# Further tiles moved between experts 15 and 16, the last norm done tile by tile, the lower bias ahead of the turned rows

## The chip, the cores and the metric

One core of a Trainium2 chip runs the whole kernel. The metric is the device time of one execution in microseconds, as the median of several runs. Engines: PE (TensorE), DVE (VectorE), ACT (ScalarE), POOL (GpSimd), SP (SyncE, which only issues DMAs here).

## The reference

One transformer layer over 256 prompt tokens and 8 sample tokens: a norm, a projection, a recurrent branch and a sparse attention branch, a merge into x, and a mixture of 32 experts; then a last norm. Only the end matters here (all float32; x is 264 rows of 1,024):

```python
def clamped_swiglu(u):
    glu = jnp.minimum(u[..., :D_FF], SWIGLU_LIMIT)
    lin = jnp.clip(u[..., D_FF:], -SWIGLU_LIMIT, SWIGLU_LIMIT)
    return glu * jax.nn.sigmoid(SWIGLU_ALPHA * glu) * (lin + 1.0)
...
    def expert_chunk(args):                      # one expert, its rows xc
        xc, e = args
        return clamped_swiglu(xc @ w_up[e] + b_up[e]) @ w_down[e] + b_down[e]
...
    return x + moe_ffn(rms_norm(x, norm_ffn), w_router, b_router, w_up, b_up, w_down, b_down)
...
    y_prompt = rms_norm(xp, norm_final)
    y_sample = rms_norm(xs, norm_final)
```

Each token goes to 4 of the 32 experts, weighted. w_up[e] is 1,024 x 2,048 (8 MB), w_down[e] 1,024 x 1,024 (4 MB).

## The kernel before

`build` runs three stages: `rwkv`, `attend`, `experts`. The first two end near 470 us. `experts` calls `expert_tiles` (L2099), in which each engine has its own program, ordered by semaphores.

**One expert.** 64 slots hold the rows of one expert. The 64 rows of 1,024 are halved over the partitions. POOL gathers the rows (`gather`, L2188), PE turns them into bank 6 (`turn_x`, L2417), DVE multiplies them by the norm's gain (`gained_x`, L2287). `up` (L2444) opens banks 0 and 1 with the bias (L2452, chosen by the one-hot tile `pick_up`), then adds eight k-steps of matmuls (L2469). DVE clamps and multiplies with ACT's sigmoid (`tile`, L2312 to L2321), PE turns the result (`turn_h`, L2425), ACT copies it to SBUF as hT (L2224). `down` (L2475) opens bank 4 with its bias (L2483) and adds eight k-steps (L2490). ACT copies bank 4 to y (`rows`, L2230). `comb` (L2431, matmuls at L2440) scatters y back over the 264 tokens into six banks, and DVE adds these to x (`adds`, L2296, at L2303). x has three tiles: 0 and 1 with 128 rows of the prompt, 2 with the 8 samples.

**Weights.** A ring of eight slots of 2,048 KB. Slots 0 to 3 hold w_up of one expert, 4 and 5 w_down of even experts, 6 and 7 of odd ones. SP issues the transfers in the order of use (L2141, L2152), each as soon as PE has used what the slot held: the first upper quarter of expert e+1 when `up(e)` is a quarter done.

**Two orders.** Up to expert 15 (`LATE` = 16) PE does up(e), turn_x(e+1), down(e-1), with comb(e-2) inside up(e). From expert 16 on it does up(e), comb(e-1), turn_x(e+1), turn_h(e), down(e), and up(e) waits for the adds of comb(e-2).

**Further tiles.** An expert with more than 64 rows has further tiles. `each` (L2119) loads their count on every engine (`more_of`, L2116, recorded at L2117), and jumps over a block (branch at L2121) if it is 0. The block holds one tile's code twice (first tile, and the loop over the others). It stands behind expert 31, and PE waits for all adds (`added` >= 192) ahead of it. In the profiled execution no instruction of the block shows up.

**Last norm.** Behind the block: DVE clears the sums; ACT squares each tile with a sum (L2268) and takes the root (L2272); DVE multiplies by the gain (L2391), forms the mean (L2395), the reciprocal (L2399) and the product (L2400); SP writes each tile out (L2177).

Of the kernel before, what the change touches and what calls it, by code (L numbers as in the profile page):

```python
# [25 lines left out]
ALU = mybir.AluOpType  # L26
# [3 lines left out]
P = 128  # L30
D = 1024
# [20 lines left out]
MORE = 16  # L52
# [52 lines left out]
def build(nc, a, o, scratch):  # L105
    ctx = ExitStack()
    with ctx:
# [73 lines left out]
        def slot_of(k):  # L181
            return pairs[k // 2][:, k % 2, :]
# [1916 lines left out]
        def expert_tiles(B, S, st, sp_routes, pool_routes, act_routes, dve_routes, pe_routes, gains, dve_routes_more, pool_routes_more, pe_routes_more):  # L2099
# [11 lines left out]
            sq_out, z = ([slot_of(3 * i + t)[:, 0:D] for t in range(3)] for i in range(2))  # L2111
            ss = sb(st, "final_ss", [P, 3])
            sq, ms, root, y_ok = (sem("fin_" + n) for n in ("squares", "ms", "root", "y_ready"))
            x_ok = Signal("fin_x_ready")
# [4 lines left out]
            def each(eng, tile, count=None, routes_more=None):  # L2119

                with eng.If((more_of(eng) if count is None else count) > 0):  # L2121
                    if routes_more is not None:
                        routes_more(eng)
                    tile(0, eng.value_load(over[0:1, MORE:MORE + 1], min_val=0, max_val=NEXP - 1), True)
                    with eng.Fori(1, MORE) as c:
                        tile(c, eng.value_load(over[0:1, bass.ds(c + MORE, 1)], min_val=0, max_val=NEXP - 1), False)

            with nc.Block() as block:
                @block.sync
                def _(sp):  # L2130
# [30 lines left out]
                    with sp.Fori(2, NEXP // 2) as pair:  # L2161
                        for half in range(2):
                            up(2 * pair + half, True)
                            down(2 * pair + half, half, True)
# [7 lines left out]
                    sp.wait_ge(S["down_done"], NEXP)  # L2172
                    each(sp, further)
                    for t, (t0, n) in enumerate(TILES):
                        sp.wait_ge(y_ok, t + 1)
# [7 lines left out]
                def _(pool):  # L2183
# [19 lines left out]
                    with pool.Fori(1, NEXP - 1) as e:  # L2203
                        gather(e + 1, e + 1, True)
# [10 lines left out]
                    pool.wait_ge(S["x_turned"], NEXP)  # L2215
                    each(pool, further, None, pool_routes_more)

                @block.scalar
                def _(act):
# [26 lines left out]
                    with act.Fori(LATE, NEXP - 1) as e:  # L2246
                        sigmoid(e)
                        turned_h(e)
                        rows(e, True)
                    sigmoid(NEXP - 1)  # L2250
                    turned_h(NEXP - 1)
                    rows(NEXP - 1, True)

# [9 lines left out]
                    each(act, further)  # L2263
                    nc.scalar.activation(root_in[:], ident[:, 0:1], ACT.Sqrt)
                    act.wait_ge(x_ok.sem, 1)

                    def squares(t, n):
                        nc.scalar.activation(sq_out[t][0:n], x[0:n, t, :], ACT.Square, accum_out=ss[0:n, t:t + 1]).then_inc(sq, 1)  # L2268

                    def rooted(t, n):  # L2270
                        act.wait_ge(ms, t + 1)
                        nc.scalar.activation(ss[0:n, t:t + 1], ss[0:n, t:t + 1], ACT.Sqrt).then_inc(root, 1)  # L2272

                    (_, n0), (_, n1), (_, n2) = TILES
                    squares(0, n0)
                    squares(1, n1)
                    rooted(0, n0)
                    squares(2, n2)
                    rooted(1, n1)
                    rooted(2, n2)  # L2280

                @block.vector
                def _(dve):
# [28 lines left out]
                    def tile(e):  # L2312
# [9 lines left out]
                        pick_upper(e + 1)  # L2322
# [21 lines left out]
                    with dve.Fori(LATE, NEXP - 1) as e:  # L2344
                        pick_lower(e)
                        tile(e)
                        gained_x(e + 1)
                        adds(e - 1, True, late_banks)
                        back(e)
                    pick_lower(NEXP - 1)  # L2350
                    tile(NEXP - 1)
                    adds(NEXP - 2, True, late_banks)
                    back(NEXP - 1)
# [32 lines left out]
                    each(dve, further, more_tiles, dve_routes_more)  # L2386
                    step = stepper(dve, dve_chain)
                    step(nc.vector.memset(ss[:], 0.0), x_ok)

                    def gained(t, n):  # L2390
                        step(nc.vector.tensor_tensor(z[t][0:n], x[0:n, t, :], gain[0:n, :], ALU.mult))  # L2391

                    def mean(t, n):
                        dve.wait_ge(sq, t + 1)
                        nc.vector.tensor_scalar(ss[0:n, t:t + 1], ss[0:n, t:t + 1], 1.0 / D, NORM_EPS, ALU.mult, ALU.add).then_inc(ms, 1)  # L2395

                    def scaled(t, n):
                        dve.wait_ge(root, t + 1)
                        step(nc.vector.reciprocal(ss[0:n, t:t + 1], ss[0:n, t:t + 1]))  # L2399
                        nc.vector.tensor_scalar(x[0:n, t, :], z[t][0:n], ss[0:n, t:t + 1], None, ALU.mult).then_inc(y_ok, 1)  # L2400

                    (_, n0), (_, n1), (_, n2) = TILES
                    gained(0, n0)
                    mean(0, n0)
                    gained(1, n1)
                    mean(1, n1)
                    scaled(0, n0)
                    gained(2, n2)
                    mean(2, n2)
                    scaled(1, n1)  # L2410
                    scaled(2, n2)

                @block.tensor
                def _(pe):
# [60 lines left out]
                    def down(e, pair, half, wait, late=False):  # L2475
                        pe.wait_ge(S["hT_ready"], e + 1)
# [31 lines left out]
                    with pe.Fori(2, LATE // 2) as pair:  # L2508
# [10 lines left out]
                    def expert(e, pair, half, more):  # L2519
                        up(e, True, 0, True)  # L2520
                        comb(e - 1, True, late_banks, e + 1)
                        if more:
                            turn_x(e + 1)
                        turn_h(e)
                        down(e, pair, half, True, True)

                    with pe.Fori(LATE // 2, NEXP // 2 - 1) as pair:
                        for half in range(2):
                            expert(2 * pair + half, pair, half, True)
                    expert(NEXP - 2, NEXP // 2 - 1, 0, True)  # L2530
                    expert(NEXP - 1, NEXP // 2 - 1, 1, False)
                    comb(NEXP - 1, True, late_banks, NEXP)
# [36 lines left out]
                    pe.wait_ge(S["added"], 6 * NEXP)  # L2569
                    each(pe, further, None, pe_routes_more)  # L2570
# [44 lines left out]
```

## Time and profile before

| | |
|---|---|
| time, median of 3 runs | 1432.77 us (1429.39 to 1432.85) |
| span of the profiled execution | 1427.3 us |
| PE busy | 1334.0 us (93%) |
| DVE, ACT, POOL busy | 495.5, 189.9, 102.5 us |
| expert matmuls, L2469 and L2490 | 462.0 and 230.2 us |
| HBM read, rate over the span | 478.60 MB, 341 GB/s |
| mean granted clock of PE | 0.981 |

The time of the profiled execution itself isn't known beside its span; the median of the runs is 5.4 us longer than the span. Times in the rows count from the start of the span. Busy shares are averages over three stages with different limits, so the rows are read by stretch. A "q" behind an engine's name is its sequencer, "ld" PE's weight load. L-numbers are lines of the kernel before.

### The profile page before, as it was taken

The numbers are of one execution on the slowest core, as the hardware profiler recorded it, in microseconds if no ns is written. First come the engines' busy times: TensorE is split into PE (matmuls) and PEld (weight loads), VectorE is DVE, ScalarE is ACT, GpSimd is POOL, SyncE is SP. The second block draws the span as 40 slices with busy tenths as digits, with TensorE's granted clock in tenths as the row PEclk, the third lists the DMA queues.
The fourth block names the chain that finished last, engine by engine and source line by source line (L and its number), as shares of the span: only waits on it lengthen the run. The fifth ranks groups of instructions, "written<-read, shape, count | busy, mean of one in ns | idle before, by whom it ended". The sixth has DMA issues, their size and how long they took to land.

```text
span 1427.3 us, 20650 instructions
## 1 busy us (share of the span) xinstructions
PE 1334.0 (93%) x8399; PEld 663.1 (46%) x8400; DVE 495.5 (35%) x1055; ACT 189.9 (13%) x407; POOL 102.5 (7%) x150
## 2 busy tenths in 40 slices
PE   6998889999899999999999999999999999999995
PEld 5887867787688533333333333333333333332331
DVE  3455556434551413223222232224222322233224
ACT  3221112323310300000000000000000000000001
POOL 1002032330000000000000000000000000000000
PEclk9999999999999899999999999999999999999998
DMA  6333248183579799999999999999999999999993
GB/s 212 121 93 92 64 104 270 60 301 111 185 256 369 310 424 430 430 430 430 431 432 430 432 430 431 430 432 427 433 432 431 431 431 432 431 432 430 432 428 141
DMA packets 87027, 479.94 MB, mean 336 GB/s; under 512 B 12740, under 2 KB 52918, under 8 KB 62008
## 3 DMA queue, kind: packets, MB, share of 16 engines
q1 hardware_dynamic: 78664, 452.00, 77.9%
q0 software_dynamic: 7600, 25.45, 5.0%
q10 hardware_dynamic: 704, 1.63, 0.3%
q8 instruction: 46, 0.75, 0.2%
q14 instruction: 13, 0.11, 0.0%
HBM read 478.60 MB, written 8.56 MB: 341 GB/s over the span
## 4 chain that ended last, share of the span: by engine, by line
PE 32%; DMA 32%; DVE 1%; ACT 1%; issue 1%; SPq 0%; DVEq 0%; ACTq 0%
DMA ring<-in_w_up 32%; PE bank L2469 19%; PE bank L2490 7%; PE bank L2440 2%; PE bank L2452 1%; PE bank L2483 1%; PE bank L2422 1%; DVE x L2303 1%; PE bank L2428 0%; PE bank L2072 0%; DVE ring L2391 0%; ACT ex_work L1901 0%; ACT x L1898 0%; DVE x L2400 0%; PE bank L238 0%
## 5 line engine op out<-in xcount | busy, mean ns | idle before, releaser
L2469 PE MATMUL bank<-ring,ex_work 128*64 128x512 f32 x2032 | 462.0, 604 | 23.0 <-DMA ring<-in_w_up 23.0
L2469 PEld LDWEIGHTS bank<-ring,ex_work 128*64 128x64 f32 x2032 | 141.2, 138 | 329.9 <-issue 285.2
L2490 PE MATMUL bank<-ring,ex_work 128*64 128x512 f32 x1024 | 230.2, 603 | 0.0
L2314 DVE TENSOR_SCALAR ex_work<-bank 128x512 f32<-128x512 f32 x32 | 22.1, 692 | 402.0 <-PE bank L2469 402.0
L2303 DVE TENSOR_TENSOR x<-bank,x 128x512 f32<-128x512 f32 (+1 forms) x192 | 117.2, 670 | 101.0 <-PE bank L2440 101.0
L2490 PEld LDWEIGHTS bank<-ring,ex_work 128*64 128x64 f32 x1024 | 71.5, 138 | 156.5 <-issue 156.5
L2440 PE MATMUL bank<-ex_work,ex_back 64*128 64x512 f32 x384 | 91.1, 606 | 1.5 <-ACT ex_work L2234 1.5
L578 PE MATMUL bank<-hT,w_group 128*128 128x264 f32 (+1 forms) x400 | 90.1, 387 | 0.0
L578 PEld LDWEIGHTS bank<-hT,w_group 128*128 128x128 f32 (+1 forms) x400 | 74.3, 186 | 14.7 <-issue 0.7
L2196 POOL DMA_INDIRECT ex_work<-scratch_h,ex_si x31 | 31.8, 1025 | 601.5 <-PE bank L2422 600.6
L2228 ACT ACTIVATE ex_work<-ex_work 128x512 f32<-128x512 f32 x32 | 20.1, 630 | 385.7 <-DVE ex_work L2314 385.7
L1381 PE MATMUL bank<-hT,w_cmp 128*128 128x264 f32 x256 | 65.3, 398 | 0.0
L2440 PEld LDWEIGHTS bank<-ex_work,ex_back 64*128 64x128 f32 x384 | 34.4, 186 | 57.8 <-issue 49.7
L2310 DVE COPY ex_pick_down<-ex_pick 64x64 f32 (+1 forms) x31 | 5.8, 188 | 159.0 <-PE bank L2490 159.0
L2234 ACT ACTIVATE ex_work<-bank 128x512 f32<-128x512 f32 x32 | 19.1, 597 | 259.4 <-PE bank L2490 259.4
L1381 PEld LDWEIGHTS bank<-hT,w_cmp 128*128 128x128 f32 x256 | 47.1, 195 | 6.8
L2483 PE MATMUL bank<-ex_bias,ex_pick_down 32*64 32x512 f32 x128 | 34.4, 612 | 15.9 <-DVE x L2303 14.5
L2224 ACT ACTIVATE ex_work<-bank 128x512 f32<-128x512 f32 x32 | 19.1, 597 | 224.9 <-PE bank L2428 224.9
L2452 PE MATMUL bank<-ex_bias,ex_pick_up 32*64 32x512 f32 x256 | 35.7, 627 | 2.5 <-DVE ex_pick_up L2306 2.5
L1810 PE MATMUL bank<-mixed,ring 128*128 128x264 f32 x128 | 30.4, 391 | 0.0
L2422 PEld LDWEIGHTS bank<-masks,ex_work 128*128 128x128 f32 x124 | 17.2, 208 | 24.4 <-issue 24.4
L1985 DVE TENSOR_TENSOR ex_work<-bank,gain_columns 128x256 f32<-128x256 f32 x64 | 23.9, 413 | 8.6 <-PE bank L2422 8.0
(489 smaller groups left out, 1189.7 us busy)
## 6 DMA issues: line engine op xcount, KB each, us to landing
ring<-in_w_up SPq DMA_DIRECT2D x127, 2048.0 KB, 23.6
ring<-in_w_down SPq DMA_DIRECT2D x64, 2048.0 KB, 26.7
w_group<-in_w_in SPq DMA_DIRECT2D x12, 1024.0 KB, 5.2
w_cmp<-in_w_in SPq DMA_DIRECT2D x8, 1024.0 KB, 9.1
ring<-in_w_out SPq DMA_DIRECT2D x8, 512.0 KB, 6.9
out_win_s<-in_state_win_kv POOLq DMA_DIRECT2D x1, 4088.0 KB, 30.7
x<-in_x_prompt SPq DMA_DIRECT2D x4, 512.0 KB, 4.9
win_rows<-in_state_win_kv SPq DMA_DIRECT2D x4, 512.0 KB, 4.9
```

The lines of the kernel that those rows point to most:

```text
L578: mm = mmul(banks[2 + i % 4][0:n, 0:T], w[:, g % 3, kc, c:c + n], hT[:, kc, :], start=(kc == 0), stop=(kc == KD - 1))
L1381: mm = mmul(gate_bank(t)[:, 0:T], w[:, t // 2 % 2, kc, P * (t % 2):P * (t % 2) + P], C["hT"][:, kc, :], start=(kc == 0), stop=(kc == KD - 1))
L1810: mmul(banks[m % 2][:, 0:T], wo(c)[:, P * m:P * m + P], mix[:, c, :], start=(c == 0), stop=False)
L1985: ins = nc.vector.tensor_tensor(B["xT"][:, :, gs], bank.rearrange("p (k s) -> p k s", k=4)[:, :, gs], R["gcol"][:, 2 * g:2 * g + 2].rearra ...
L2196: pool.indirect_dma_start(B["xg"][:], None, halves(scratch["h"]), bass.IndirectOffsetOnAxis(ap=B["si"][:, 0:1], axis=0), bounds_check=last ...
L2303: nc.vector.tensor_tensor(dst, banks[bank][0:n, :], dst, ALU.add).then_inc(S["added"], 1)
L2422: mm = nc.tensor.transpose(banks[6][:, P * k:P * k + P], B["xg"][:, 256 * (k // 2):256 * (k // 2) + 256].rearrange("s (p c) -> s c p", c=2 ...
L2440: mm = mmul(banks[bank], B["back"][hs, P * t:P * t + P], B["y"][hs, :], start=True, stop=True)
L2452: mmul(banks[n // 2][lo:lo + SLOTS, :], B["pick_up"][es, :], B["bias"][es, 512 * n:512 * n + 512], start=True, stop=False)
L2469: mm = mmul(banks[n // 2][lo:lo + SLOTS, :], B["xT"][:, k % 4, SLOTS * (k // 4):SLOTS * (k // 4) + SLOTS], (ninth[:, k, :] if e_ninth and ...
L2483: mmul(banks[4][SLOTS * n:SLOTS * n + SLOTS, :], B["pick_down"][0:NEXP, :], B["bias"][0:NEXP, 2 * FF + 512 * n:2 * FF + 512 * n + 512], st ...
L2490: mm = mmul(banks[4][SLOTS * n:SLOTS * n + SLOTS, :], B["hT"][:, k % 4, SLOTS * (k // 4):SLOTS * (k // 4) + SLOTS], slot_of(8 + 4 * half + ...
```

## The change

1. The block of further tiles moves from behind expert 31 to between experts 15 and 16, on every engine. For that the pipeline is emptied there: comb(15) and its adds come ahead of it, turn_x(16), the pick and the gain of expert 16 behind it. The loops of the first half end an expert or a pair earlier and the rest is written out. Inside the branch, each engine also waits for the last further tile.
2. The last norm: DVE's memsets (sums, and a tile with eps) move ahead of expert 31. Tiles go in the order 2, 0, 1, each from its own two adds on. ACT squares, and takes the root with the mean and eps in its scale and bias. DVE takes the reciprocal, and for tiles 0 and 1 one operation x * r * gain. For tile 2, POOL multiplies by the gain and ACT scales. SP writes tiles 0, 2, 1.
3. In `down`, the wait for hT comes behind the bias matmuls.
4. ACT's root table load comes ahead of the last `rows`; the last experts of both halves don't pick the next one's upper bias.

```diff
--- SP
-                    with sp.Fori(2, NEXP // 2) as pair:
...
-                    sp.wait_ge(S["down_done"], NEXP)
-                    each(sp, further)
+                    def ring_empty(sp):
+                        sp.wait_ge(S["down_done"], LATE)
...
+                    pairs_of_experts(2, LATE // 2)
+                    each(sp, further, None, ring_empty, ring_empty_again)
+                    pairs_of_experts(LATE // 2, NEXP // 2)
+                    for t in (0, 2, 1):
+                        t0, n = TILES[t]
+                        sp.wait_ge(y_ok[t], 1)
--- POOL
-                    with pool.Fori(1, NEXP - 1) as e:
+                    with pool.Fori(1, LATE - 1) as e:
                         gather(e + 1, e + 1, True)
...
+                    pool.wait_ge(S["x_turned"], LATE)
+                    each(pool, further, None, pool_routes_more, rows_taken)
+                    with pool.Fori(LATE - 1, NEXP - 1) as e:
+                        gather(e + 1, e + 1, True)
+                    (_, n2) = TILES[2]
+                    pool.wait_ge(S["added"], 6 * (NEXP - 1) + 2)
+                    nc.gpsimd.tensor_tensor(z, x[0:n2, 2, :], gain[0:n2, :], ALU.mult).then_inc(z_ok, 1)
--- ACT
                     each(act, further)
+                    with act.Fori(LATE, NEXP - 1) as e:
+                        sigmoid(e)
+                        turned_h(e)
+                        rows(e, True)
+                    sigmoid(NEXP - 1)
+                    turned_h(NEXP - 1)
                     nc.scalar.activation(root_in[:], ident[:, 0:1], ACT.Sqrt)
+                    rows(NEXP - 1, True)
+                    act.wait_ge(eps_ok, 2)
+                    for i, t in enumerate((2, 0, 1)):
+                        n = TILES[t][1]
+                        act.wait_ge(S["added"], 6 * (NEXP - 1) + 2 * i + 2)
                         nc.scalar.activation(sq_out[t][0:n], x[0:n, t, :], ACT.Square, accum_out=ss[0:n, t:t + 1]).then_inc(sq, 1)
+                        act.wait_ge(sq, i + 1)
+                        nc.scalar.activation(ss[0:n, t:t + 1], ss[0:n, t:t + 1], ACT.Sqrt, bias=eps[0:n, 0:1], scale=1.0 / D).then_inc(root, 1)
+                    act.wait_ge(z_ok, 1)
+                    act.wait_ge(s_ok, 1)
+                    nc.scalar.activation(x[0:TS, 2, :], z, ACT.Copy, scale=ss[0:TS, 2:3]).then_inc(y_ok[2], 1)
--- DVE
-                    with dve.Fori(3, LATE) as e:
+                    with dve.Fori(3, LATE - 1) as e:
...
+                    adds(LATE - 3, True, early_banks)
+                    back(LATE - 2)
+                    tile(LATE - 1, False)
+                    pick_lower(LATE - 1)
                     adds(LATE - 2, True, late_banks)
                     back(LATE - 1)
...
                     more_tiles = more_of(dve)
-                    adds(NEXP - 1, True, late_banks)
-                    dve.wait_ge(S["added"], 6 * NEXP)
+                    adds(LATE - 1, True, late_banks)
+                    dve.wait_ge(S["added"], 6 * LATE)
...
                     each(dve, further, more_tiles, dve_routes_more)
+                    pick_upper(LATE)
+                    gained_x(LATE)
+                    pick_lower(LATE)
+                    tile(LATE)
+                    gained_x(LATE + 1)
+                    back(LATE)
...
+                    for i, t in enumerate((2, 0, 1)):
+                        n = TILES[t][1]
+                        dve.wait_ge(root, i + 1)
+                        if t == 2:
+                            nc.vector.reciprocal(ss[0:n, t:t + 1], ss[0:n, t:t + 1]).then_inc(s_ok, 1)
+                        else:
+                            step(nc.vector.reciprocal(ss[0:n, t:t + 1], ss[0:n, t:t + 1]))
+                            dve.wait_ge(S["added"], 6 * NEXP)
+                            nc.vector.scalar_tensor_tensor(x[0:n, t, :], x[0:n, t, :], ss[0:n, t:t + 1], gain[0:n, :], ALU.mult, ALU.mult).then_inc(y_ok[t], 1)
--- PE
                     def down(e, pair, half, wait, late=False):
-                        pe.wait_ge(S["hT_ready"], e + 1)
...
                                  start=True, stop=False)
+                        pe.wait_ge(S["hT_ready"], e + 1)
...
+                    up(LATE - 2, True, 2)
+                    turn_x(LATE - 1, True)
+                    down(LATE - 3, LATE // 2 - 2, 1, True)
+                    up(LATE - 1, True, 2)
+                    pe.wait_ge(S["added"], 6 * (LATE - 2))
+                    down(LATE - 2, LATE // 2 - 1, 0, True)
                     comb(LATE - 2, True, late_banks, LATE)
                     turn_h(LATE - 1)
                     down(LATE - 1, LATE // 2 - 1, 1, True, True)
...
+                    comb(LATE - 1, True, late_banks, LATE)
...
-                    pe.wait_ge(S["added"], 6 * NEXP)
-                    each(pe, further, None, pe_routes_more)
+                    pe.wait_ge(S["added"], 6 * LATE)
+                    each(pe, further, None, pe_routes_more, sums_taken)
...
+                    turn_x(LATE)
+                    expert(LATE, LATE // 2, 0, True, False)
+                    expert(LATE + 1, LATE // 2, 1, True)
+                    with pe.Fori(LATE // 2 + 1, NEXP // 2 - 1) as pair:
```

## Rows read from the trace of the kernel before

**Rows 1.** The page's chain that ended last, by line (share of the span)

```profile
DMA ring<-in_w_up 32%; PE bank L2469 19%; PE bank L2490 7%; PE bank L2440 2%; PE bank L2452 1%; PE bank L2483 1%; PE bank L2422 1%; DVE x L2303 1%; PE bank L2428 0%; PE bank L2072 0%; DVE ring L2391 0%; ACT ex_work L1901 0%; ACT x L1898 0%; DVE x L2400 0%; PE bank L238 0%
```

**Rows 2.** Table by stretches: stretch, length, busy us (instructions) of each engine, clock, DMA share, GB/s

```profile
900.00:950.00 50.00, 46.87 (x214) 15.48 (x212) 12.46 (x26) 3.62 (x6) 1.39 (x3) 0.97 1.01 431
...
1200.00:1395.00 195.00, 183.11 (x848) 60.20 (x844) 47.45 (x98) 11.54 (x19) 6.03 (x10) 0.98 1.01 431
```

**Rows 3.** Timeline of PE: start, us, engine, line, operation, count, idle before and its releaser

```profile
488.09 16.61 PE L2469 MATMUL bank<-ring,ex_work 128*64 128x512 f32 x64
...
906.65 5.25 PE L2469 MATMUL bank<-ring,ex_work 128*64 128x512 f32 x16 [1.66 <-DMA ring<-in_w_up]
...
939.64 1.07 PE L2483 MATMUL bank<-ex_bias,ex_pick_down 32*64 32x512 f32 x4 [0.69 <-ACT ex_work L2224]
...
948.68 13.95 PE L2469 MATMUL bank<-ring,ex_work 128*64 128x512 f32 x64
...
967.52 1.07 PE L2483 MATMUL bank<-ex_bias,ex_pick_down 32*64 32x512 f32 x4 [0.95 <-DVE x L2303]
...
976.56 13.95 PE L2469 MATMUL bank<-ring,ex_work 128*64 128x512 f32 x64
...
1099.03 3.65 PE L2469 MATMUL bank<-ring,ex_work 128*64 128x512 f32 x16 [0.44 <-DMA ring<-in_w_up]
```

**Rows 4.** L2141's transfers of 952:953 and of 980:981; DMA issues (KB each, us to landing)

```profile
L2141 SPq DMA_DIRECT2D ring<-in_w_up x1: 332/332/332, 952.5 to 952.5; - x1
...
DMA to landing us min/median/max: 13.0/13.0/13.0
...
DMA to landing us min/median/max: 14.9/14.9/14.9
...
w_group<-in_w_in SPq DMA_DIRECT2D x12, 1024.0 KB, 5.2
```

**Rows 5.** Lines L2121 and L2117: instructions, ns min/median/max, first and last start

```profile
L2121 DVEq COMPARE_BRANCH  x1: 67/67/67, 1416.8 to 1416.8; - x1
L2121 PEldq COMPARE_BRANCH  x1: 3462/3462/3462, 1417.7 to 1417.7; - x1
...
L2117 PEldq TENSOR_LOAD <-overflow x1: 486/486/486, 1416.8 to 1416.8; - x1
```

**Rows 6.** Table by stretches, as rows 2, behind PE's last matmul

```profile
1415.00:1418.00 3.00, 0.00 (x0) 0.00 (x0) 2.30 (x5) 0.47 (x1) 0.00 (x0) 1.00 0.00 0
1418.00:1421.00 3.00, 0.00 (x0) 0.00 (x0) 2.90 (x6) 2.94 (x8) 0.00 (x0) 0.58 0.03 8
```

**Rows 7.** Timeline of all engines behind the last upper weights, as rows 3

```profile
1395.07 3.65 PE L2469 MATMUL bank<-ring,ex_work 128*64 128x512 f32 x16 [0.86 <-DMA ring<-in_w_up]
...
1401.64 0.74 PE L2428 MATMUL bank<-masks,ex_work 128*128 128x128 f32 x4
...
1403.07 1.07 PE L2483 MATMUL bank<-ex_bias,ex_pick_down 32*64 32x512 f32 x4 [0.69 <-ACT ex_work L2224]
...
1411.86 2.85 PE L2440 MATMUL bank<-ex_work,ex_back 64*128 64x512 f32 x12 [0.70 <-ACT ex_work L2234]
...
1413.10 3.67 DVE L2303 TENSOR_TENSOR x<-bank,x 8x512 f32<-8x512 f32 x6 [7.25 <-PE bank L2440]
...
1417.53 1.06 ACT L2268 ACTIVATE ring<-x 128x1024 f32<-128x1024 f32 x1 [3.85 <-DVE final_ss L2388]
...
1418.49 0.19 ACT L2268 ACTIVATION_READ_ACCUMULATOR ring<-x 128x1 f32 x1
...
1418.86 1.22 DVE L2391 TENSOR_TENSOR ring<-x,ffn_gain 128x1024 f32<-128x1024 f32 x1
...
1424.15 0.35 SPq L2177 DMA_DIRECT2D out_y_s<-x  x1
```

**Rows 8.** Groups of POOL by line (busy, mean ns); waits of SP, 900:1100 (us, times, longest)

```profile
L722 POOL TENSOR_TENSOR m_X<-m_X,masks 128x512 f32<-128x512 f32 x2 | 3.2, 1602 | 0.2
...
SPq L2141 <- PE bank L2469: 163.8, 27, 17.1
```

More of the change, by code:

```diff
@@ L2110, in expert_tiles, with each @@
             sums = ((0, 2), (0, 3), (1, 5), (1, 6), (2, 7), (2, 0))
[L2111 to L2114, printed above, removed]
+            sq_out, z = [slot_of(t)[:, 0:D] for t in range(3)], slot_of(3)[0:TS, 0:D]
+            ss, eps = sb(st, "final_ss", [P, 3]), sb(st, "final_eps", [P, 1])
+            sq, root, z_ok, s_ok, eps_ok = (sem("fin_" + n) for n in ("squares", "roots", "sample_gained", "sample_scale", "eps"))
+            y_ok = [sem(f"fin_y_ready{t}") for t in range(3)]
             def more_of(eng):
                 return eng.value_load(over[0:1, 0:1], min_val=0, max_val=MORE)
-            def each(eng, tile, count=None, routes_more=None):
+            def each(eng, tile, count=None, routes_more=None, done=None):
                 with eng.If((more_of(eng) if count is None else count) > 0):
@@ L2126, in each @@
                         tile(c, eng.value_load(over[0:1, bass.ds(c + MORE, 1)], min_val=0, max_val=NEXP - 1), False)
+                    if done is not None:
+                        done(eng)
             with nc.Block() as block:
@@ L2160, in _, with pairs_of_experts @@
                     down(3, 1, True)
-                    with sp.Fori(2, NEXP // 2) as pair:
-                        for half in range(2):
-                            up(2 * pair + half, True)
-                            down(2 * pair + half, half, True)
+                    def pairs_of_experts(lo, hi):
+                        with sp.Fori(lo, hi) as pair:
+                            for half in range(2):
+                                up(2 * pair + half, True)
+                                down(2 * pair + half, half, True)
                     def further(c, e, first):
@@ L2214, in further, with rows_taken @@
                         pool.wait_ge(x_in, 16 * (c + 1))
[L2215 to L2216 removed]
+                    def rows_taken(pool):
+                        pool.wait_ge(x_turned, MORE)
+                    pool.wait_ge(S["x_turned"], LATE)
[5 more added lines that the diff above has]
+                    nc.gpsimd.tensor_tensor(z, x[0:n2, 2, :], gain[0:n2, :], ALU.mult).then_inc(z_ok, 1)
                 @block.scalar
@@ L2386, in _ @@
                     each(dve, further, more_tiles, dve_routes_more)
-                    step = stepper(dve, dve_chain)
[L2388 to L2411, printed above, removed]
+                    pick_upper(LATE)
[4 more added lines that the diff above has]
+                    back(LATE)
+                    with dve.Fori(LATE + 1, NEXP - 1) as e:
+                        pick_lower(e)
+                        tile(e)
+                        gained_x(e + 1)
+                        adds(e - 1, True, late_banks)
+                        back(e)
@@ L2507, in _ @@
                     down(2, 1, 0, True)
-                    with pe.Fori(2, LATE // 2) as pair:
+                    with pe.Fori(2, LATE // 2 - 1) as pair:
                         up(2 * pair, True, 2)
@@ L2517, in _ @@
                     down(LATE - 1, LATE // 2 - 1, 1, True, True)
[L2519 to L2532, printed above, removed]
+                    comb(LATE - 1, True, late_banks, LATE)
                     def further(c, e, first):
@@ L2568, in further, with sums_taken, expert @@
                         mm.then_inc(comb_ok, 1)
-                    pe.wait_ge(S["added"], 6 * NEXP)
-                    each(pe, further, None, pe_routes_more)
+                    def sums_taken(pe):
+                        pe.wait_ge(added, 6 * MORE)
+                    pe.wait_ge(S["added"], 6 * LATE)
+                    each(pe, further, None, pe_routes_more, sums_taken)
+                    def expert(e, pair, half, more, behind=True):
+                        up(e, True, 0, True)
+                        if behind:
+                            comb(e - 1, True, late_banks, e + 1)
+                        if more:
+                            turn_x(e + 1)
+                        turn_h(e)
+                        down(e, pair, half, True, True)
+                    turn_x(LATE)
+                    expert(LATE, LATE // 2, 0, True, False)
+                    expert(LATE + 1, LATE // 2, 1, True)
+                    with pe.Fori(LATE // 2 + 1, NEXP // 2 - 1) as pair:
+                        for half in range(2):
+                            expert(2 * pair + half, pair, half, True)
+                    expert(NEXP - 2, NEXP // 2 - 1, 0, True)
+                    expert(NEXP - 1, NEXP // 2 - 1, 1, False)
+                    comb(NEXP - 1, True, late_banks, NEXP)
         rwkv()
```

45 lines of the change are left out of this document (12 added, 33 removed).

## Prediction

> **What bounds the kernel now.** I read the chain of waits first: in the expert stage it alternates between weight transfers and TensorE work [rows 1]. The table by stretches says which of the two sets the end: from 900 to 1395 us (first and last of the five stretches stand here, the others move 430 to 432 GB/s) the 16 DMA engines are busy all the time, while PE has gaps [rows 2]. A transfer of 2,048 KB (2.097 MB) takes 2.097 MB / 431 GB/s = 4.87 us of that stream, an expert (six of them) 29.2 us. So the stage ends when the bytes are in, plus what follows the last upper transfer. A microsecond in which the DMA engines have nothing to do is lost for good; one in which PE waits is not, as long as transfers are queued. After the last upper weights only latency is left: PE's last up block starts at 1395.07, the final DMA is issued at 1424.15 and the span ends at 1427.35 [rows 7]. The change works at both places: it shortens the second and puts an extra stall of PE into the first. The median of the runs is 1432.77 us, 5.4 us above the span of the profiled execution; all differences below are made on its trace and then added to the median.
>
> **PE's slack in the middle.** At expert 16 PE already runs late. Its up block starts at 948.68; SP can refill the first upper slot only when that quarter is used, at 952.5, and the transfer lands 13.0 us later [rows 3, 4]. What is queued ahead of it is 13.0 us less what a transfer takes on an empty queue. For that I take the loads of w_in, issued one by one: 1,024 KB land after 5.2 us [rows 4]. Less their bytes at 431 GB/s (2.4 us) 2.8 us are fixed, so 2,048 KB take 4.9 + 2.8 = 7.7 us. The slack in the DMA queue at that moment is 13.0 - 7.7 = 5.3 us. The Trainium skill, DMA: Bandwidth & Descriptors, section on the cost components, gives a fixed 2.0 us plus bytes at 436 GB/s, which would make 6.8 us, a slack of 6.2 us, and the loss below 0.9 us smaller; the w_in row is above that (by the page 4.4 us, measured 5.2).
>
> **The moved block: how late PE gets.** Overflow is zero here: after the last expert no line of the further tiles (L2193 to L2568) has an instruction, each engine only loads the count and jumps. Before, PE did this at 1416.8, when nobody waited for it. Now everything queued behind it on PE is turn_x(16), and then expert 16. Step by step from the end of down(15), which was at 947.7 (the bias of up(16), 1.0 us, comes between it and 948.68):
> - turn_x(16), four transposes like turn_h's 0.74 us in the tail [rows 7], is no longer ahead of down(14): 0.7 us earlier. The lower bias of expert 15 goes under ACT's copy of hT, for which PE waited 0.69 us [rows 3]. down(15) ends at 947.7 - 1.4 = 946.3.
> - comb(15) must now come first: 0.7 us of waiting for the copy of y, as in the tail [rows 7], so comb starts at 947.0 and takes PE 2.8 us. DVE's first add starts 1.24 us behind comb's start and the six end 3.67 us later, as in the tail (1411.86, 1413.10) [rows 7]: 951.9.
> - PE waits for `added` >= 96, loads the count (0.49 us; from its start to the branch 0.87 us) and branches over the block. That branch took 3.46 us on PE, against 0.07 on DVE [rows 5]. In the old place it costs nothing. PE goes on at 956.35.
> - turn_x(16) 0.7 us; the bias of up (1.0 us) covers DVE's gains: up(16) starts at 958.1 instead of 948.7.
> So up(17)'s first transfer is issued 9.4 us later. The branch is the term I know least: it is one row, from a time with an idle DMA system. Its ends: 0.07 us (DVE's) and some 7 us (twice the row, an estimate). I take the row. The Trainium skill, Runtime: NRT & Kernel Launch, section Instruction fetch mechanics, says that a taken branch whose target is outside the sequencer's window has to fetch the target by DMA before anything goes on; by that rule it recurs wherever the block stands, since the distance is the same, and without that stall the loss below would be 3.4 us smaller.
>
> PE is idle from 949.8 to 956.35. The granted clock fell to half speed 3.8 us after PE's last matmul of the kernel (at 1.00 from 1415 to 1418, 0.58 from 1418 to 1421) [rows 6], and it was low when PE resumed at 906.65 after 1.7 us of waiting: 16 matmuls took 5.25 us instead of 3.65 [rows 3]. One such dip costs 1.6 us. A longer one, at the start of the experts, costs 2.7 us in the up block at 488.09 (16.61 us against 13.95) [rows 3]. I take 2.3 us, with ends at 1.6 and 3.6 (the long one with a us more, for the bias in front of it), for the idle time is much longer than at 906.
>
> **Sum in the middle.** 9.4 + 2.3 - 5.3 = 6.4 us in which the DMA engines have nothing queued. The later issues have room: expert 17 to 18 had 14.9 us at 980.4 [rows 4]. There PE is later by another stretch: without comb(15) in expert 16 nothing hides DVE's clamp and product behind up(16), so turn_h waits 2.9 us (1398.72 to 1401.64 in the tail [rows 7]); up(17) starts near 987.0 instead of 976.56, 10.4 us later, less the 6.4 by which transfers are later too: 14.9 - 4.0 = 10.9 us, above 7.7. PE's backlog then shrinks: an expert takes it 27.9 us (948.68 to 976.56) against 29.2 or more for the DMA. Before, PE first waits again at 1099.03, expert 21 [rows 3]. The added backlog of 4.0 us takes 3 or 4 experts more at 1.3 us each, so it is gone by expert 25, before the end. SP's count load and branch come while it waits for a slot (it waits for PE's up blocks up to 17.1 us at once) [rows 8]; POOL's gather of expert 16 waits for turn_x(15), an expert earlier; DVE's branch takes 0.07 us. All are hidden; were SP's jump as long as PE's, it would still fit. The pick and gain of expert 16 behind the block on DVE wait for PE in any case.
>
> **The tail.** From the last up block:
> - The bias of down(31) no longer waits for hT: turn_h ends at 1402.38 and the bias runs to 1403.4 with ACT's copy under it; before, it started at 1403.07 and took 1.07 us [rows 7]. Gain 0.7 us. In other late experts it gains nothing: there the bias waits for DVE's first add (0.95 us, 967.52), not for hT [rows 3].
> - comb then starts at 1411.15, the adds end at 1416.05; tile 2 is done after two, at 1413.6, tile 0 after four, at 1414.85.
> - Squares (1.06 us), the accumulator's read (0.19) and the root, of one column like the read (0.2), go tile by tile on ACT, each about 1.4 us: tile 2 at 1413.7, tile 0 at 1415.1, tile 1 at 1416.4, root 1 at 1417.8. The 0.7 us between the last add and the old memset and first square (1416.77 to 1417.53) are gone, the mean is in the root, and the gain of tiles 0 and 1 is in the final operation.
> - On DVE, a reciprocal (one column, some 0.2 us) and the one fused operation, which the trace doesn't have at this size; the gain multiply over 1,024 columns takes 1.22 us [rows 7]: I take 1.23, with 2.4 as the far end. Tile 0 ends at 1417.9, tile 1 at 1419.3.
> - Tile 2's product is on POOL. Its products of 512 columns took 1.6 us [rows 8], so 3.2 us here, done at 1417.0; ACT scales it by 1418.9, behind root 1. All beside the other work.
> - The last DMA is y_p's second, issued at 1419.4 instead of y_s at 1424.15. It needs a little longer to land (512 KB, 1.2 us of bytes, against 32 KB): 4.75 - 0.15 = 4.6 us gained, the bias included. Bounds: 3.3 (the fused operation at half rate) to 5.0.
>
> **Sum.** 6.4 - 4.6 = +1.8 us on 1432.8: 1434.6. About 0.3% (4.3 us) is what a measurement of this kernel can tell from no change; this lies within it.
>
> **The rivals.**
> - *The stall stays covered* (faster). For it: the other engines jump in under 0.1 us, and PE's 3.46 us may be special to the end of the program. With a branch of 0.1 us and one dip of 1.6 us the middle costs 6.0 + 1.6 - 5.3 = 2.3 us, net -2.3: 1430.5. Without the dip and with 1 us less of latency it costs nothing: 1428.2. Against: the row is plain. 0.27, of which 0.13 beyond 4.3 us.
> - *PE's jump waits for its code behind the weights* (slower). It now happens with the DMA engines full, where 2 MB transfers hold them. Every us over 3.46 is a us of idle DMA. From 6.0 us on the kernel is over 0.3% slower (4.3 - 1.8 = 2.5 more); with 7 us it costs 3.5 more: 1438.1. Against: no row shows PE waiting for code anywhere under full load. 0.18.
> - *The tail gains less*, since tile 1's chain over ACT and DVE is dependent: 1.3 us less (3.3), 1435.9. 0.08.
> - The forecast itself: 0.47, with its own range 1431.5 to 1437.5 (branch by 1 us, dip 1.6 to 3.6, tail 4 to 5).
>
> **How the numbers follow.** Faster by over 0.3% 0.13; slower 0.19 (0.17 of the second rival and 0.02 of others); within 0.68. The range leaves out the full cover and a jump over 7.5 us: 1428.9 to 1438.6.
>
> **What would show it.** In the trace of the changed kernel: PE's branch at L2121 near 952 with 3 to 4 us; a stretch near 960 to 967 in which the DMA engines move under half of 431 GB/s; a first upper transfer of expert 17 that lands 7 to 8 us after its issue; the last up block later by that same gap, 6.4 us; then from its end to the last output DMA 20.7 instead of 25.4 us. The prediction is wrong if the branch is short, if the DMA engines never go idle, or if the distance from the last up block to the end isn't 4 to 5 us less.

## The result: slower by 0.5%, and the profile after

The changed kernel takes 1438.41 us (median of 5 runs, 1437.19 to 1447.19), the kernel before in the same comparison 1432.77 (1429.39 to 1434.59). The ratio is 1.0052 with a 95% interval of 1.0032 to 1.0073, so +7.5 us, between 4.6 and 10.5; the forecast was +1.8. The execution that was profiled is the one of 1447.19 us, span 1445.3. 8 us of that lie ahead of anything that the change touches: its first up block of the experts starts at 496.04, that of before at 488.09. In the ten kept traces that block starts anywhere from 488.1 to 496.0 us. Below I therefore compare distances inside the expert stage, not clock times. All comparisons by time leave out a single slow execution, one of 3089.77 us among the twelve of "The tail alone" below.

PE around expert 16 (timeline, as rows 3, which answer it with 939.64 to 976.56):

```profile
956.06 2.85 PE L2454 MATMUL bank<-ex_work,ex_back 64*128 64x512 f32 x12 [0.70 <-ACT ex_work L2256]
971.35 1.01 PE L2436 MATMUL bank<-masks,ex_work 128*128 128x128 f32 x4 [12.45 <-issue]
972.29 1.99 PE L2466 MATMUL bank<-ex_bias,ex_pick_up 32*64 32x512 f32 x8
974.21 15.53 PE L2483 MATMUL bank<-ring,ex_work 128*64 128x512 f32 x64
989.66 0.74 PE L2436 MATMUL bank<-masks,ex_work 128*128 128x128 f32 x4
992.66 0.74 PE L2442 MATMUL bank<-masks,ex_work 128*128 128x128 f32 x4 [2.25 <-DVE ex_work L2336]
```

comb(15) ends at 958.9, and PE then does nothing for 12.45 us. "issue" means that the profile shows no semaphore that held it; in fact its sequencer, which hands it its instructions, waited for the adds, loaded the count and branched. Where the time went is in the sequencer's rows (line L2121: operation, ns, first and last start; rows 5 of before have 3462 ns in the old place):

```profile
L2121 SPq COMPARE_BRANCH  x1: 50/50/50, 914.5 to 914.5; - x1
L2121 ACTq COMPARE_BRANCH  x1: 54/54/54, 956.2 to 956.2; - x1
L2121 DVEq COMPARE_BRANCH  x1: 67/67/67, 961.0 to 961.0; - x1
L2121 PEldq COMPARE_BRANCH  x1: 6185/6185/6185, 961.9 to 961.9; - x1
```

PE's branch takes 6.19 us. It ends at 968.1, but the turning matmuls come only at 971.35: another 3.3 us. The DMA engines meanwhile run dry (table by stretches: stretch, busy us of PE, PEld, DVE, ACT, POOL, clock, DMA share, GB/s; rows 2 had 431):

```profile
963.00:966.00 3.00, 0.00 (x0) 0.00 (x0) 0.00 (x0) 0.00 (x0) 0.00 (x0) 0.63 0.88 369
966.00:969.00 3.00, 0.00 (x0) 0.19 (x1) 0.00 (x0) 0.00 (x0) 0.00 (x0) 0.50 0.43 175
969.00:972.00 3.00, 0.65 (x4) 0.61 (x3) 0.00 (x0) 0.00 (x0) 0.00 (x0) 0.50 0.00 0
972.00:975.00 3.00, 3.00 (x12) 0.60 (x12) 0.85 (x3) 0.00 (x0) 1.03 (x1) 0.50 0.08 18
...
978.00:981.00 3.00, 3.00 (x18) 0.98 (x16) 0.00 (x0) 0.00 (x0) 0.00 (x0) 1.00 0.37 71
```

The exact size of the hole comes from the landings. The last transfer that was queued (L2154) and the next one (L2143; rows 4 have 952.5 and 13.0 for it):

```profile
L2154 SPq DMA_DIRECT2D ring<-in_w_down x1: 333/333/333, 943.2 to 943.2; - x1
...
DMA to landing us min/median/max: 26.0/26.0/26.0
...
L2143 SPq DMA_DIRECT2D ring<-in_w_up x1: 332/332/332, 979.6 to 979.6; - x1
...
DMA to landing us min/median/max: 7.7/7.7/7.7
```

943.2 + 26.0 = 969.2 and 979.6 + 7.7 = 987.3: 18.1 us between two landings that are 4.9 us apart in a full stream. So the stream of weights loses 13.2 us.

The tail (timeline behind the last up block; rows 7):

```profile
1423.62 0.75 PE L2442 MATMUL bank<-masks,ex_work 128*128 128x128 f32 x4
...
1424.29 1.07 PE L2496 MATMUL bank<-ex_bias,ex_pick_down 32*64 32x512 f32 x4
...
1434.33 3.67 DVE L2318 TENSOR_TENSOR x<-bank,x 8x512 f32<-8x512 f32 x6 [6.59 <-PE bank L2454]
...
1435.69 2.34 POOL L2238 TENSOR_TENSOR ring<-x,ffn_gain 8x1024 f32<-8x1024 f32 x1 [69.16 <-DVE x L2318]
1435.70 1.06 ACT L2290 ACTIVATE ring<-x 8x1024 f32<-8x1024 f32 x1 [2.67 <-DVE x L2318]
...
1440.17 1.29 DVE L2425 SCALAR_TENSOR_TENSOR x<-x,final_ss,ffn_gain 128x1024 f32<-128x1024 f32 x1
...
1441.48 0.35 SPq L2191 DMA_DIRECT2D out_y_p<-x  x1
```

The bias directly follows turn_h, the first square starts while DVE still adds, and the last output DMA is issued 20.8 us behind the last up block (which ended at 1420.7), against 25.4 before (1398.72 to 1424.15). This last DMA carries 512 KB instead of 32 and needs 3.9 us to the end of the span instead of 3.2.

So inside the expert stage: 13.2 lost, 4.6 gained, 0.7 given back at the landing: +9.3 us. From the first up block to the end of the span it is 949.3 against 939.3 us, +10.0. The timed runs say +7.5 (4.6 to 10.5).

### The profile page after: what moved, and what is told of

Its sections match the earlier page's. It is cut to its first block, busy times and chain, and to the rows that moved or that the text cites. A ratio compares the mean times of both kernels' runs of the same rounds, so it can differ in the third digit from the quotient of the medians.

```text
span 1445.3 us, 20604 instructions
## 1 busy us (share of the span) xinstructions
PE 1344.0 (93%) x8399; PEld 670.0 (46%) x8400; DVE 491.2 (34%) x1048; ACT 191.3 (13%) x408; POOL 104.4 (7%) x151
## 4 chain that ended last, share of the span: by engine, by line
PE 42%; DMA 21%; DVE 2%; issue 1%; ACT 0%; DVEq 0%; SPq 0%; ACTq 0%
PE bank L2483 23%; DMA ring<-in_w_up 21%; PE bank L2504 10%; PE bank L2454 3%; PE bank L2466 1%; PE bank L2496 1%; PE bank L2436 1%; DVE x L2318 1%; PE bank L2442 0%; PE bank L2072 0%; PE bank L2065 0%; DVE x L2425 0%; ACT ring L2290 0%; DVE ex_work L2333 0%; DVE ex_work L2336 0%
## 5 line engine op out<-in xcount | busy, mean ns | idle before, releaser
L2436 PE MATMUL bank<-masks,ex_work 128*128 128x128 f32 x124 | 23.4, 312 | 14.0 <-issue 12.4
```

What stands on the lines that cost most here:

```text
L2436: mm = nc.tensor.transpose(banks[6][:, P * k:P * k + P], B["xg"][:, 256 * (k // 2):256 * (k // 2) + 256].rearrange("s (p c) -> s c p", c=2 ...
```

## The experiments

My theory once the trace was seen: all of the loss is PE's jump over the block, at a moment when PE already runs late and the transfer queue has only 5.3 us of slack; all of the gain is in the tail and doesn't need the move. The rivals: the drained pipeline is the cost, not the jump; another engine's jump is; the tail needs the block out of the way. A "hole" below is the time between two landings of weights, less the 4.9 us of a full stream.

**The tail alone.** The kernel before with the block at its place, and from the change the last norm, the memsets, the table load and this edit:

```diff
                     def down(e, pair, half, wait, late=False):
-                        pe.wait_ge(S["hT_ready"], e + 1)
...
+                        pe.wait_ge(S["hT_ready"], e + 1)
                         for j in range(2):
```

> The block of further tiles stays behind expert 31 as before; only the last norm by tiles, the early memsets and table load, and the lower bias ahead of hT are taken from the change. Theory (the loss is all in the middle, the gain all in the tail): no idle stretch of the DMA engines, 20.7 to 20.9 us instead of 25.4 from the end of the last up block to the last output DMA, so 4.6 us faster than before. Rival (the tail's gain needs the block out of the way, since DVE and ACT have to jump over it first): at most 2 us faster.

Measured: ratio 0.9993 (0.9980 to 1.0006), 1431.52 us against 1433.16. No idle stretch of the DMA engines in the middle. But the tail is 23.3 us, between the two expectations. Its trace says why (timeline of ACT):

```profile
1419.91 1.28 ACT L2279 ACT_TABLE_LOAD   x1 [2.65 <-DVE x L2307]
...
1421.20 1.06 ACT L2279 ACTIVATE ring<-x 8x1024 f32<-8x1024 f32 x1
...
1422.37 1.28 ACT L2281 ACT_TABLE_LOAD   x1
```

Behind the block the program loads ACT's table again, although the block isn't run and a root has been computed ahead of it: once for the square, once for the root, 2.56 us on the path. In the changed kernel, where no block stands between that root and the squares, there is no such second load. That the sigmoids inside the block are the reason is my reading; no run takes them out. In the kernel before, a root whose result nobody uses (the "warming root") stood directly behind the block and took the load up, beside the adds. I had moved it ahead of the block, as the change has it, where it no longer helps.

**The tail alone, one table load.** The same with the warming root behind the block:

```diff
                     sigmoid(NEXP - 1)
                     turned_h(NEXP - 1)
-                    nc.scalar.activation(root_in[:], ident[:, 0:1], ACT.Sqrt)
                     rows(NEXP - 1, True)
...
                     each(act, further, None, None, all_added)
+                    nc.scalar.activation(root_in[:], ident[:, 0:1], ACT.Sqrt)
                     act.wait_ge(eps_ok, 2)
```

> As tail_block_end, with ACT's root table loaded behind the block instead of ahead of the last copy of bank 4. Theory (behind a block that may hold sigmoids ACT loads its table again, twice 1.28 us on the path): one load, done before the first two adds; 20.8 us from the last up block to the last output DMA, 4.6 us faster than before. Rival (the loads are no loss, the rest of the tail is slower beside POOL or the block's jump): still 23.3 us.

Measured: 1428.02 us against 1431.71, ratio 0.9966 (0.9951 to 0.9982), 4.9 us faster (2.6 to 7.0). Of the versions that still handle an overflow this is the only one that is clearly faster than the kernel before. Its timeline:

```profile
1415.45 1.28 ACT L2274 ACT_TABLE_LOAD   x1 [0.37 <-issue]
1416.38 3.67 DVE L2307 TENSOR_TENSOR x<-bank,x 8x512 f32<-8x512 f32 x6 [6.60 <-PE bank L2434]
...
1417.75 1.06 ACT L2279 ACTIVATE ring<-x 8x1024 f32<-8x1024 f32 x1 [0.80 <-DVE x L2307]
...
1423.53 0.35 SPq L2180 DMA_DIRECT2D out_y_p<-x  x1
```

The load lies beside comb and the first adds; the last up block ended at 1402.8, so the tail is 20.8 us, as in the changed kernel. The rival, that the block has to be out of the way, falls: ACT and POOL need no add to load the count and jump, and DVE's 0.7 us hide behind ACT's first root.

**The move alone.** The changed kernel with the last norm and the wait in `down` of before.

> The block moves between experts 15 and 16 as in the change; the last norm and the order of bias and hT are those of before. Theory: PE is out for its jump of 6 us and a second wait of 3 us, the DMA engines go idle for some 13 us, so 13 us slower than before. Rival (the stall costs what was forecast, 6.4 us, and the rest of the measured difference lies elsewhere): 6 to 8 us slower.

Measured: 1443.11 us against 1433.16, ratio 1.0081 (1.0056 to 1.0106), 11.6 us slower (8.0 to 15.2). The hole between two landings is 13.3 us, PE's branch 6145 ns. The loss is in the move, and is of the size that the landings give. Here two of the four turning matmuls of expert 16 come directly behind the branch, which ends at 958.4, and the second stall stands between them and the other two (timeline of PE):

```profile
958.44 0.70 PE L2452 MATMUL bank<-masks,ex_work 128*128 128x128 f32 x2 [9.18 <-issue]
961.75 0.70 PE L2452 MATMUL bank<-masks,ex_work 128*128 128x128 f32 x2 [2.61 <-issue]
```

**The drained order without the block.** The calls of `each` are left out on all engines; for PE:

```diff
                     pe.wait_ge(S["added"], 6 * LATE)
-                    each(pe, further, None, pe_routes_more, sums_taken)
```

> The change with the calls of the further tiles' block left out on every engine, the drained order around expert 16 kept. It leaves out what an overflow would need; these inputs have none. Theory (PE's jump does it): PE is late by 9.4 - 0.9 - 3.5 = 5.0 us plus a clock dip of 0 to 1.6, against a slack of 5.3, so 0 to 1.3 us of idle DMA, and with the tail's 4.6 us 3.3 to 4.6 faster than before. Rival (the drained pipeline does it, the comb and adds of expert 15 and the missing cover in expert 16): 4 us slower or more, like the change.

Measured: 1429.98 us against 1433.16, ratio 0.9987 (0.9967 to 1.0006). That is 1.9 us faster, with an interval from 4.7 faster to 0.9 slower: it doesn't tell the expected 3.3 us from none, but it excludes the rival's +4. The trace is plain: from 950 to 975 us 423 GB/s, and no landing in the middle is late by more than 1.1 us.

**The block on all engines but PE.** Only the line above is left out.

> The change with the block's call left out on PE alone; SP, POOL, ACT and DVE load the count and jump. Leaves out PE's part of an overflow, of which these inputs have none. Theory: as without the block on any engine, 3.3 to 4.6 us faster than before. Rival (a jump of SP or DVE holds the transfers or PE up): several us slower than the kernel without any block.

Measured: 1427.89 us, ratio 0.9968 (0.9949 to 0.9987), 4.6 us faster. No cost of the jumps of SP, POOL, ACT and DVE can be seen (first up block to end of span 934.9 us, against 935.4 without any block); PE's alone turns -4.6 into +7.5. PE around expert 16 (timeline):

```profile
946.56 2.85 PE L2454 MATMUL bank<-ex_work,ex_back 64*128 64x512 f32 x12 [0.70 <-ACT ex_work L2256]
951.53 0.75 PE L2436 MATMUL bank<-masks,ex_work 128*128 128x128 f32 x4 [2.12 <-DVE x L2318]
952.45 1.09 PE L2466 MATMUL bank<-ex_bias,ex_pick_up 32*64 32x512 f32 x8 [0.17 <-DVE ex_pick_up L2321]
953.47 13.95 PE L2483 MATMUL bank<-ring,ex_work 128*64 128x512 f32 x64
```

The first transfer behind the drained order (its issue line and the time to landing):

```profile
L2143 SPq DMA_DIRECT2D ring<-in_w_up x1: 333/333/333, 957.3 to 957.3; - x1
...
DMA to landing us min/median/max: 7.8/7.8/7.8
```

The drain costs 2.12 us of waiting for the adds, at full clock (13.95 us for the up block). The transfer lands 7.8 us after its issue, as on an empty queue (7.7), and the longest hole in the middle is 0.8 us: the drain alone uses up the 5.3 us of slack and hardly more. Whatever comes on top, comes out of the end of the kernel.

**The jump by itself.** The kernel before, nothing drained, with one more jump on PE between down(15) and up(16):

```diff
+                    with pe.If(more_of(pe) > 0):
+                        for q in range(152):
+                            nc.tensor.matmul(banks[3][:, 0:2 * P], ident, masks[:, 0:2 * P], start=True, stop=True)
                     with pe.Fori(LATE // 2, NEXP // 2 - 1) as pair:
```

skip_near has 8 in place of 152. I count four instructions for such a matmul.

> The kernel before, with one more count load and branch on PE alone between down(15) and up(16), over 8 matmuls that never run; nothing is drained. Theory (the price is that of fetching code outside the buffered stretch): the branch takes some 0.1 us, up(16) is 1 us later. Rival (a taken branch costs several us whatever its distance): 3 to 6 us.

> As skip_near, over 152 matmuls (608 instructions, about the size of the further tiles' block on PE). Theory: the branch takes 6 us with the DMA engines full, perhaps 3 more behind it for the next piece of code; PE late by 7 to 10 us against a slack of 5.3, so 2 to 5 us of idle DMA. Rival (distance doesn't matter, or the drained order made the long jump of the changed kernel): under 1 us, no idle DMA.

One execution each, 1437.68 and 1433.72 us, too few for a comparison by time, and the first starts its experts 6.5 us later than the second; the traces decide. From the first up block to the end of the span skip_near takes 940.7 us and skip_far 943.3, against 939.3 before. The branches of skip_near and skip_far:

```profile
L2527 PEldq COMPARE_BRANCH  x1: 219/219/219, 950.7 to 950.7; - x1
```

```profile
L2527 PEldq COMPARE_BRANCH  x1: 5879/5879/5879, 943.3 to 943.3; - x1
```

0.22 against 5.88 us: distance decides, the drained order has no part in it. The near jump doesn't make up(16) late at all, not even by the 1 us expected: the sequencer loads the count and jumps while the matmuls of down(15) still run, and the bias follows them at once (timeline of skip_near):

```profile
947.19 7.09 PE L2490 MATMUL bank<-ring,ex_work 128*64 128x512 f32 x32
954.21 1.09 PE L2452 MATMUL bank<-ex_bias,ex_pick_up 32*64 32x512 f32 x8
```

Behind the far jump PE again stands for a second time, and works at half clock (timeline of skip_far):

```profile
954.76 1.98 PE L2452 MATMUL bank<-ex_bias,ex_pick_up 32*64 32x512 f32 x8 [7.85 <-issue]
956.68 15.78 PE L2469 MATMUL bank<-ring,ex_work 128*64 128x512 f32 x64
```

The branch runs from 943.3 to 949.2 and down(15) until 946.9, so of the 7.85 us in which PE stands only 2.3 belong to the branch; the bias starts 5.5 us after its end. The hole is 4.1 us with nothing drained, within the 2 to 5 expected. The same kernel's other jump, at the end of the program with idle DMA engines, took 3.49 us.

**Half the distance.** The changed kernel without PE's loop copy of the block.

> The changed kernel with PE's loop over the further tiles left out of the block (the first tile's code stays; an overflow of more than one tile would need the rest, these inputs have none): the distance of the jump is about half. Theory (any target outside the buffered stretch costs its fetch, however far): 6 us again, idle DMA 10 to 13 us. Rival (the price grows with the distance): 3 us, idle DMA 7 to 10 us.

One execution, 1439.62 us. Its timeline of PE:

```profile
958.87 0.75 PE L2436 MATMUL bank<-masks,ex_work 128*128 128x128 f32 x4 [3.40 <-issue]
959.55 1.37 PE L2466 MATMUL bank<-ex_bias,ex_pick_up 32*64 32x512 f32 x4
964.77 1.97 PE L2466 MATMUL bank<-ex_bias,ex_pick_up 32*64 32x512 f32 x4 [3.85 <-issue]
```

Neither expectation holds: the branch takes neither 6 us nor 3, and the 9.4 us of the hole are what the rival gave, but for another reason. The branch itself takes 0.36 us, from 958.5 to 958.8: the target was already there. But in the middle of the bias matmuls, eight of which should run as one, PE stands 3.85 us without a semaphore to wait for. It goes on 6.0 us after the branch's end, which is as long as a far branch takes in the stream; 2 of these us it had work for. So there are two fetches that occur apart: that of a target that isn't there yet, and that of the next piece of code behind the target, for which no packet runs until after the jump.

**All traces side by side.** One execution each; the hole is the longest one behind 900 us.

| kernel | first up block to the end, us | against before | hole, us |
|---|---|---|---|
| before | 939.3 | | 0.7 |
| changed | 949.3 | +10.0 | 13.2 |
| tail_block_end | 938.1 | -1.2 | 0.7 |
| tail_one_table | 934.6 | -4.7 | 0.7 |
| move_only | 951.6 | +12.3 | 13.3 |
| drain_no_block | 935.4 | -3.9 | 0.8 |
| all_but_pe | 934.9 | -4.4 | 0.8 |
| skip_near | 940.7 | +1.4 | 0.7 |
| skip_far | 943.3 | +4.0 | 4.1 |
| one_copy | 944.2 | +4.9 | 9.4 |

## Why the prediction was wrong

It forecast +1.8 us and no measurable change; +7.5 was measured, and both kernels' traces give +9 to +10. That the measured median still lies just inside the stated range (up to 1438.6) is luck: the cost that the traces show would lie outside. By its steps:

- **What bounds, and the slack: right.** A transfer on an empty queue was worked out at 7.7 us from w_in; measured 7.7 and 7.8. The slack of 5.3 us fits all_but_pe: PE late by about as much, and a hole of only 0.8 us. The fixed 2.0 us that the prediction quotes from the Trainium skill, DMA: Bandwidth & Descriptors, stand there as a fit to transfers issued by GpSimd; SP issues these, and their measured 7.7 us decide.
- **Drain: right.** From comb(15)'s start to up(16)'s start all_but_pe takes 6.9 us (946.56 to 953.47); the forecast, less the count load and the branch, was 958.1 - 947.0 - 4.3 = 6.8.
```profile
q1 hardware_dynamic: 103, 1.46, 93.0%
q14 instruction: 1, 0.01, 0.5%
```

```profile
q1 hardware_dynamic: 42, 0.56, 53.5%
q8 instruction: 1, 0.02, 2.2%
```

- **The second stall: missing altogether.** 3.3 us between the branch's end and the first matmul. The prediction priced one fetch. In the trace of before nobody waited for a second one, since nothing but the program's end stood behind the jump, but its packet was there to be seen, 0.8 us after the branch's end (DMA table of before, 1421.2 to 1424; the branch ends at 1421.1):

```profile
q8 instruction: 1, 0.02, 3.7%
```

Under "bounds" I doubled the row to 7 us; the true end, branch and second stall, is 9.5 us. The second stall is again a packet of q8: in the changed kernel it starts at 968.8, when the engines have already run dry, in skip_far at 952.5, in the full stream (DMA tables of the changed kernel, 968.1 to 971.4, and of skip_far, 949.2 to 952.5 and 952.5 to 953.5):

```profile
q1 hardware_dynamic: 7, 0.03, 2.4%
q8 instruction: 1, 0.02, 2.2%
```

```profile
q1 hardware_dynamic: 101, 1.43, 100.9%
```

```profile
q1 hardware_dynamic: 27, 0.44, 106.0%
q8 instruction: 1, 0.02, 6.1%
```

All these fetches together, each one packet of 16 KB (in us; the wait counts from the branch's start, for a next piece from the branch's end):

| fetch | weights | wait for the packet's start | from there until it goes on |
|---|---|---|---|
| target, five at the program's end | none | 1.0 to 1.1 | 2.3 to 2.7 |
| target: changed, move_only, skip_far | full stream | 3.8, 3.8, 3.5 | 2.4, 2.4, 2.3 |
| next piece: changed, move_only | run dry or nearly so | 0.7, 1.1 | 2.6, 2.2 |
| next piece: skip_far, one_copy | full, or nearly so | 3.3, 3.5 | 2.3, 2.4 |

The far targets alone would leave a rival, that the place in the program makes the difference, for all idle cases lie at its end. The next pieces answer it: all four lie in the middle of the kernel, and the wait is 3.3 to 3.5 us with weights in flight and 0.7 to 1.1 without. So the second stall is short in the changed kernel because the first has already emptied the stream.

- **The clock: nearly right.** 2.3 us taken; measured 1.01 - 0.74, 1.99 - 1.09 and 15.53 - 13.95 us, together 2.8.
- **The sum in the middle.** 6.4 forecast. 6.4 + 2.7 + 3.3 + 0.5 = 12.9, measured 13.2 in the landings. The two terms of the jump make up the error.
- **The hand-over to expert 18: right; the backlog: longer than forecast, without a price.** turn_h waits 2.25 us in expert 16 (2.9 forecast, of which turn_x covers the rest), no second hole over 1 us follows, and PE first waits for its last upper quarter again at 1327.88, expert 28 instead of 25, still before the end.
- **The tail: right in size, 20.8 us for 20.7 forecast.** POOL needed 2.34 us where 3.2 were taken, the fused operation 1.29 for 1.23. What was too small is the landing of the last DMA, 0.7 us more and not 0.15, so 4.0 us net instead of 4.6.

By the Trainium skill, Runtime: NRT & Kernel Launch, section Instruction fetch mechanics, code comes in blocks, the next one fetched while the current one runs, and a taken branch to a target outside them has to wait for a fetch by DMA. The traces agree: over 8 matmuls the branch took 0.22 us and over 152 5.88, with a packet of PE's instruction queue ahead of its end.

What stays open: by what rule the DMA engines let the code's packet wait among those of the weights, why PE in move_only stops two matmuls behind the target and in the changed kernel at once (where the target lies in its piece of code wasn't looked at), and why the timed difference is under what the traces give (+7.5 against +9 to +10; the interval holds both).

## What to carry to other kernels

Moving "dead" code is not free where it is jumped over: look at the branch's row on each engine, price it in the load of the new place, and count two fetches, that of the target and that of the next piece of code behind it. What the engine still has queued when its sequencer reaches the branch covers part of the price; behind a wait that empties the engine, as here, nothing does. A stall of a compute engine that is not the bottleneck costs only beyond the slack of the transfer queue; that slack can be read from the time between issue and landing less the time on an empty queue. And ask of each part of a change whether it needs the others: here the gain in the tail came without the move.

## What the runs showed of the hardware

- A taken branch on PE over 152 matmuls (some 600 instructions by my count) or over the block: 3.4 to 3.7 us with idle DMA engines, 5.9 to 6.2 us with some 430 GB/s of weights in flight; over 8 matmuls 0.22 us; over about half of the block 0.36 us.
- The next piece of code comes only after the jump: PE went on 3.3 (changed kernel), 3.4 (move_only), 5.5 (skip_far) and 6.0 us (one_copy) after the branch's end, the first two with the stream run dry or nearly so, the others with weights in flight. In move_only and one_copy it had 0.7 and 2 us of work in that time.
- The difference is the wait of one 16 KB packet for its start, 0.7 to 1.1 us on idle DMA engines and 3.3 to 3.8 us among the weights.
- PE's sequencer made the near jump of skip_near while matmuls issued before it still ran; it cost PE no time.
- SP, ACT, DVE and POOL jumped over their parts of the same block in 0.05 to 0.07 us, with weights in flight too. Their parts have far fewer instructions than PE's; whether that is the reason wasn't tried.
- Behind a block that is jumped over ACT loaded its table again, 1.28 us each for the square and for the root; with a root first it was one load.
